# A chunked linear-attention stage: one list of steps over all heads in place of a loop over heads

## The reference, cut to what matters

```python
z = p[..., O_GA:O_RW] @ lp['w_gla_gate'] + lp['b_gla_gate']
la = (jax.nn.log_sigmoid(z.astype(f32)) / GLA_GATE_TAU)
def step(S, inp):                      # one chunk of 64 tokens
    qi, ki, vi, li = inp
    b = jnp.cumsum(li, axis=2)
    bl = b[:, :, -1:, :]
    qe = qi * jnp.exp(b)
    A = jnp.einsum('bhcd,bhsd->bhcs', qe, ki * jnp.exp(-b))
    A = jnp.where(mask, A, 0.0)
    o = jnp.einsum('bhcd,bhde->bhce', qe, S) + jnp.einsum('bhcs,bhse->bhce', A, vi)
    S = jnp.exp(bl[:, :, 0, :])[..., None] * S + jnp.einsum('bhsd,bhse->bhde', ki * jnp.exp(bl - b), vi)
    return S, o
og = og * lax.rsqrt(jnp.mean(og * og, axis=-1, keepdims=True) + GLA_NORM_EPS)
og = og.reshape(B, T, GLA_VW).astype(h.dtype) * lp['g_gla_norm'] * jax.nn.silu(gg)
```

## Time and profile before

| | us |
|---|---|
| median of 3 runs | 5423.79 |
| lowest, highest | 5419.95, 5428.64 |
| the profiled execution | 5427.57 |
| its span, first to last instruction | 5425.8 |
| from the first instruction of gla to the first of rwkv | 356.1 |

### The profile page before, as it was taken

How to read it: one execution, slowest core, us unless ns; L and a number is a source line. 1 busy time by engine, 2 the same in 40 slices (tenths; PEclk the granted TensorE clock), 3 DMA queues, 4 the chain that set the end, 5 groups by cost and what they waited for, 6 DMA issues and landing times. The chain is left out here.

```text
span 5425.8 us, 80977 instructions
## 1 busy us (share of the span) xinstructions
PE 4506.1 (83%) x30972; PEld 3060.4 (56%) x30972; DVE 3376.8 (62%) x6700; ACT 1090.8 (20%) x2093; POOL 1667.9 (31%) x1412
## 2 busy tenths in 40 slices
PE   8899998665887778799797764999899999999980
PEld 1899997553666667565387763444344443434430
DVE  0423332334555555311297664999999999999998
ACT  2100000332333333212433322011110111010101
POOL 0000000000111111000013334666566566656666
PEclk9999999667988888899898877999999999999985
DMA  5222222212000000231402224999999999999998
GB/s 221 83 94 94 93 91 102 73 67 67 24 24 28 24 24 19 102 122 59 151 25 79 76 71 162 394 378 378 339 384 375 367 359 379 386 344 384 362 348 299
DMA packets 354226, 1010.83 MB, mean 186 GB/s; under 512 B 39486, under 2 KB 120318, under 8 KB 349410
## 3 DMA queue, kind: packets, MB, share of 16 engines
q0 software_dynamic: 156672, 570.49, 26.9%
q1 hardware_dynamic: 197228, 435.98, 22.5%
HBM read 902.35 MB, written 103.99 MB: 185 GB/s over the span
## 5 line engine op out<-in xcount | busy, mean ns | idle before, releaser
L2611 PE MATMUL peer_v_b<-peer_vt,peer_mix 128*128 128x512 f32 x2048 | 943.1, 615 | 127.1 <-DVE peer_mix L2448 82.2
L2599 PE MATMUL peer_s_b<-dense_hT_d,peer_ut 128*128 128x512 f32 x2048 | 900.9, 593 | 51.5 <-DMA peer_G2s<-mod 51.5
L2384 POOL DMA_INDIRECT peer_ring<-in_peer_v,peer_idx x544 | 717.2, 1318 | 291.1 <-issue 160.6
L2611 PEld LDWEIGHTS peer_v_b<-peer_vt,peer_mix 128*128 128x128 f32 x2048 | 401.9, 198 | 652.5 <-issue 498.4
L2378 POOL DMA_INDIRECT peer_ring<-in_peer_u,peer_idx x544 | 597.3, 1098 | 487.4 <-DVE peer_acc L2500 229.9
L1367 POOL TENSOR_TENSOR rw_An<-rw_abT,rw_join 128x256 f32<-128x256 f32 x160 | 126.1, 795 | 1934.2 <-DVE rw_abT L1277 1545.0
L2599 PEld LDWEIGHTS peer_s_b<-dense_hT_d,peer_ut 128*128 128x128 f32 x2048 | 389.7, 190 | 542.0 <-issue 490.3
L2500 DVE SCALAR_TENSOR_TENSOR peer_acc<-peer_ring,peer_coef,peer_acc 128x1024 f32<-128x1024 f32 x534 | 653.9, 1279 | 0.0
L2537 DVE CUSTOM_DVE_ANT_0 peer_ring<-peer_ring,peer_h 128x1024 f32<-128x1024 f32 x544 | 637.2, 1218 | 2.0 <-DVE peer_h L2514 1.0
L56 PE MATMUL proj_acc<-proj_hT_high,proj_w_low 128*128 128x352 f32 x1584 | 512.3, 323 | 25.6 <-DVEq L363 25.6
L57 PE MATMUL proj_acc<-proj_hT_low,proj_w_high 128*128 128x352 f32 x1584 | 508.7, 321 | 0.0
(11 more groups left out here) (418 smaller groups left out, 6816.1 us busy)
## 6 DMA issues: line engine op xcount, KB each, us to landing
peer_ut<-in_peer_ut SPq DMA_DIRECT2D x128, 512.0 KB, 9.9
peer_vt<-in_peer_v SPq DMA_DIRECT2D x128, 512.0 KB, 8.0
pT<-proj_o SPq DMA_DIRECT2D x66, 528.0 KB, 3.0
proj_w<-in_w_in SPq DMA_DIRECT2D x66, 512.0 KB, 4.2
G<-route_G SPq DMA_DIRECT2D x16, 2048.0 KB, 16.4
peer_gt<-G SPq DMA_DIRECT2D x128, 256.0 KB, 6.0
mod_w<-in_w_ada SPq DMA_DIRECT2D x12, 2048.0 KB, 8.3
peer_ring<-in_peer_u,peer_idx POOLq DMA_INDIRECT x544, 10.3
```

Of the source, the lines that this page charges most:

```text
L2384: pool.indirect_dma_start(out=ring[:, k, :], out_offset=None, in_=t["peer_v"], in_offset=bass.IndirectOffsetOnAxis(ap=idx[U % 2][:, k:k + ...
L2599: last = pe.matmul(s_b[:, n % 3, :], ut[:, n % UT, k, :], hT_d[:, k, :], start=(k == 0), stop=(k == KD - 1))
L2611: last = pe.matmul(v_b[:, m % 4, :], mix[:, part % 2, e, tokens], vt[:, part % 2, e, cols], start=(e == 0), stop=(e == PART - 1))
```

## The change

The GLA stage becomes one list of steps over all four heads, made by `gla_steps` from a string of letters, and all four engines go through that same list, each taking the steps that it has a part in. Five streams are woven: t (turn a tile), s (its states), o (its output), p (the next head's preparation) and e (the last head's samples and end). Between the tiles of head h stand the preparation of head h + 1 and samples, sums of squares, root and og of head h - 1; head 0's preparation comes ahead, head 3's end behind. The list for a middle head, read out of the string:

```diff
+GLA_ORDER = (
+    "eptepstoestoepetspoeetesoeteseepoetesetepososeop",
+)
+def gla_steps():
+    def prepare(h):
+        return ([("z", h, g) for g in range(3)] + [(kind, h, 0) for kind in ("soft", "sums", "exps", "expand")]) if h < GH else []
+    def end(h):
+        if h < 0:
+            return []
+        return ([("turn", h, TILES), ("o", h, TILES), ("ks", h, 0)] + [("ss", h, b) for b in range(NB)] + [("sq", h, 0)]
+                + [("ms", h, g) for g in range(3)] + [("rstd", h, 0), ("og", h, 0)])
+    def stream(which, h):
+        return {"t": [("turn", h, i) for i in range(TILES)], "s": [("st", h, i) for i in range(TILES)],
+                "o": [("o", h, i) for i in range(TILES)], "p": prepare(h + 1), "e": end(h - 1)}[which]
+    relative = lambda which, h: [(kind, head - h, x) for kind, head, x in stream(which, h)]
+    whole = {which: iter(relative(which, 1)) for which in "tsope"}
+    turns = [(which, next(whole[which])) for which in "".join(GLA_ORDER)]
+    steps = prepare(0)
+    for h in range(GH):
+        have = {which: relative(which, h) for which in "tsope"}
+        steps += [(kind, head + h, x) for which, (kind, head, x) in turns if (kind, head, x) in have[which]]
+    return steps + end(GH - 1)
...
-        vg_next = s.sb("vg_next", [P, 4, M])
-        v, gate = s.sb("v", [P, 2, M]), s.sb("gate", [P, 2, M])
+        vg = [s.sb(f"vg{n}", [P, 4, M]) for n in range(2)]
         S_in = s.sb("S_in", [P, NB, GV])
         S_out = s.sb("S_out", [P, NB, GV])
         z = s.sb("z", [P, M])
         sp_ = s.sb("softplus", [P, M])
         B = s.sb("B", [P, M])
         up, dn, rest = s.sb("exp_up", [P, M]), s.sb("exp_down", [P, M]), s.sb("exp_rest", [P, M])
-        ends = s.sb("ends", [P, SEQ // GC + NB])
-        qe, ke, k2 = s.sb("qe", [P, M]), s.sb("ke", [P, M]), s.sb("k2", [P, M])
+        ends = s.sb("ends", [P, 2, SEQ // GC + NB])
+        qe, ke, k2 = ([s.sb(f"{name}{n}", [P, M]) for n in range(2)] for name in ("qe", "ke", "k2"))
         S = s.sb("S", [P, 4, GV])
-        kv = s.sb("kv", [P, 2, 3 * P])
+        kv, kv_s = s.sb("kv", [P, 3, 3 * P]), s.sb("kv_s", [NS, 3 * P])
         k2s = s.sb("k2s", [NS, NB, P])
         at = s.sb("at", [P, 2, P])
-        o, og = s.sb("o", [P, 2, M]), s.sb("og", [P, 2, M])
+        o = [s.sb(f"o{n}", [P, 2, M]) for n in range(2)]
+        og = s.sb("og", [P, 2, M])
+        sq, sig, rstd = s.sb("sq", [P, 2, M]), s.sb("sig", [P, 2, M]), s.sb("rstd", [P, M])
         ones = s.sb("ones", [P, P])
         eps = s.sb("eps", [P, 1])
-        sq = s.sb("sq", [P, 2 * M])
-        zb = s.ps("zb", [P, 3, 512])
-        at_b = s.ps("at_b")
-        turn_b = s.ps("turn_b")
-        o_b = s.ps("o_b")
-        s_b = [s.ps(f"s_b{n}") for n in range(2)]
-        N = TILES + 1
+        tb, o_b, s_b = (s.ps(name, [P, 2, 512]) for name in ("tb", "o_b", "s_b"))
+        zb, at_b = s.ps("zb"), s.ps("at_b")
...
+        def turned_kv(h, i):
+            return kv[:, (h * TILES + i) % 3, :] if i < TILES else kv_s
+        def kv_before(h, i):
+            if i == TILES:
+                return (h - 1, TILES) if h else None
+            n = h * TILES + i - 3
+            return divmod(n, TILES) if n >= 0 else None
...
+                sp.dma_start(gaT[:, :], t["gaT"]).then_inc(consts_in, 16)
+                sp.dma_start(wz[:, :, :], t["w_gate"].rearrange("h r p -> r h p")).then_inc(consts_in, 16)
+                sp.dma_start(cst[:, :, :], t["gla_cst"].rearrange("h p n -> p h n")).then_inc(consts_in, 16)
+                sp.dma_start(starts[:, :], t["starts"][:, 0:M].broadcast_to([P, M])).then_inc(consts_in, 16)
                 load_qk(0)
                 load_vg(0)
+                for dst, name in ((ident, "ident"), (mask, "gla_mask"), (mask_s, "gla_mask_s"), (seq_rows, "seq_rows")):
+                    sp.dma_start(dst[:, :], t[name]).then_inc(consts_in, 16)
+                load_vg(1)
                 load_states(0)
-                with sp.Fori(0, GH - 1) as h:
-                    head(h, True)
-                head(GH - 1, False)
-                sp.wait_ge(stored, 16 * 2 * GH)
+                sp.wait_ge(scaled, 3)
+                load_qk(1)
+                for h in range(GH):
+                    if h:
+                        sp.wait_ge(S_ready, state_at(h - 1, CH + NB - 1))
+                        sp.dma_start(t["new_gla_s"][h - 1], S_out[:, :, :]).then_inc(s_stored, 16)
+                        sp.wait_ge(o_summed, upto("o", h - 1, TILES))
+                        load_states(h)
+                        sp.wait_ge(og_ready, h)
+                        sp.dma_start(t["ogT"][h - 1], og[:, :, :]).then_inc(og_stored, 16)
+                        if h + 1 < GH:
+                            load_vg(h + 1)
+                    if h + 2 < GH:
+                        sp.wait_ge(scaled, 3 * (h + 2))
+                        load_qk(h + 2)
+                    sp.wait_ge(S_ready, state_at(h, CH - 1))
+                    sp.dma_start(t["new_gla_p"][h], S[:, CH % 4, :]).then_inc(p_stored, 16)
+                sp.wait_ge(S_ready, state_at(GH - 1, CH + NB - 1))
+                sp.dma_start(t["new_gla_s"][GH - 1], S_out[:, :, :]).then_inc(s_stored, 16)
+                sp.wait_ge(og_ready, GH)
+                sp.dma_start(t["ogT"][GH - 1], og[:, :, :]).then_inc(og_stored, 16)
...
+                    elif kind == "turn":
+                        n = upto("turn", h, x) - 1
+                        rows = P if x < TILES else NS
+                        act.wait_ge(turned, n + 1)
+                        before = kv_before(h, x)
+                        if before:
+                            act.wait_ge(o_summed, upto("o", *before))
+                            act.wait_ge(s_summed, last_state(*before))
+                        act.copy(turned_kv(h, x)[0:rows, :], tb[0:rows, n % 2, 0:3 * P]).then_inc(kv_ready, 1)
+                    elif kind == "o":
+                        n = upto("o", h, x) - 1
+                        rows = P if x < TILES else NS
+                        act.wait_ge(o_summed, n + 1)
+                        if h >= 2:
+                            act.wait_ge(og_ready, h - 1)
+                        act.copy(o[h % 2][:, :, x * P:x * P + rows],
+                                 o_b[:, n % 2, 0:2 * rows].rearrange("p (a c) -> p a c", a=2)).then_inc(o_ready, 1)
+                    elif kind == "sq":
+                        act.wait_ge(o_ready, upto("o", h, TILES))
+                        if h:
+                            act.wait_ge(ms_summed, 3 * h)
+                        act.activation(sq[:, :, :], o[h % 2][:, :, :], ACT.Square).then_inc(squares_ready, 1)
+                    elif kind == "ms":
+                        act.wait_ge(ms_summed, 3 * h + x + 1)
+                        if h:
                             act.wait_ge(og_ready, h)
-                        if i == 0:
-                            act.copy(gate[:, :, :], vg_next[:, 2:4, :]).then_inc(gate_kept, 1)
-                        if more and i in PREP:
-                            prep(PREP[i], h + 1)
-                    copy_o(h, N - 1)
-                    act.wait_ge(o_ready, h * N + N)
-                    act.activation(sq[:, :], o[:, :, :].rearrange("p a m -> p (a m)"), ACT.Square).then_inc(squares_ready, 1)
-                    if more:
-                        act.wait_ge(S_ready, (h + 1) * (US + 1))
-                        expand(h + 1)
-                    act.wait_ge(ms_summed, h + 1)
-                    ch.link(act.activation(z[:, :].rearrange("p (g c) -> p g c", g=3), zb[:, :, 0:G3], ACT.Ln, bias=eps[:, :]))
-                    act.activation(z[:, :], z[:, :], ACT.Exp, scale=-0.5)
-                    act.wait_ge(gate_kept, h + 1)
-                    act.activation(sq[:, :], gate[:, :, :].rearrange("p a m -> p (a m)"), ACT.Sigmoid).then_inc(rstd_ready, 1)
-
-                def copy_o(h, i):
-                    act.wait_ge(o_summed, h * N + i + 1)
-                    rows = P if i < TILES else NS
-                    act.copy(o[:, :, i * P:i * P + rows],
-                             o_b[:, 0:2 * rows].rearrange("p (a c) -> p a c", a=2)).then_inc(o_ready, 1)
-
-                prep("softplus", 0)
-                prep("exps", 0)
-                expand(0)
-                ch.enter(0, 3)
-                head(0, True, True)
-                ch.leave(1)
-                with act.Fori(1, GH - 1) as h:
-                    ch.enter(h - 1, 3)
-                    head(h, False, True)
-                    ch.leave(GH - 2)
-                head(GH - 1, False, False)
+                        act.activation(rstd[:, g_cols(x)], zb[:, 0:G3], ACT.Ln,
+                                       bias=eps[:, :]).then_inc(ms_read, 1)
+                    elif kind == "rstd":
+                        act.wait_ge(ms_read, 3 * (h + 1))
+                        act.activation(rstd[:, :], rstd[:, :], ACT.Exp, scale=-0.5)
```

(54 more changed lines are left out.)

378 lines of the change are left out of this document (151 added, 227 removed).

## The result

The changed kernel takes 5377.94 us (median of 4 runs, 5371.03 to 5384.10) against 5421.87 for the kernel before on the same chip (4 runs, 5408.24 to 5428.64): a ratio of 0.9922, 95% interval 0.9898 to 0.9945. The forecast was 5359, range 5325 to 5410, faster at 0.9. So the sign and the range hold, and of the 65 us of gain forecast 44 came.

The account below looks back on a forecast made before the run. Waits, and a slower TensorE clock after them, were taken to bound the stage. Its terms, 37.5 + 37.4 + 63.6 + 63.6 + 51.2 + 37.8 = 291 against 356.1 us, gain 65: 5359 us, range 5325 to 5410.

Parts of the forecast that it names:

- Start: Stage start up to the first head's first turn: from 31.9 to about 37.5 us, waiting for const loads behind 2.1 MB more.
- Head 0: First head, its tiles cleared of most other work: 31 us at the high clock level, 47 at the low, 37.4 taken.
- The point two fifths of the way from the fast end: Clock level chosen between the all-high sum of 256 us and the all-low 343 for the stage: 291.
- Heads 1 and 2: Middle heads carrying all five streams: 54 us each at the high clock level, 78 at the low, 63.6 taken.
- (a): ScalarE at a middle head's boundary: copy, rstd, sigmoid, then exponentials; 10 us without an output copy, o7 needing o5's bank.
- (b): VectorE's og at a middle head's boundary, after the sigmoid: 7.5 us, with expand and the next head's masks behind it.
- (c): SP's v and gate loads for the next head, issued only behind og: about 10.7 us before its first turn.
- The tail: Last head's samples' output, ms, rstd, og and store: today's 37.8 us, three-part ms saving a wait, paying two round trips.
- Rival 1: TensorE stays at 1.2 GHz nearly throughout the stage: 13 us less, 5411, covering 5395 to 5420; chance 0.13.
- Table loads: ScalarE's two loads ahead of og: 1.28 us each by the row; the skill's 2.66 would add 2.8 per boundary.
- 3: Rival: the streams do not run beside each other, stalls only move; stage 325, gain 31 us, 5393; chance 0.16.
- 2: Rival: v/gate loads at two head boundaries make it slower, at 23 us each and low clock 5435; chance 0.05.

Follow-up runs that it names:

- kernel tail: Changed kernel with mask loads ahead of q, k, v and gate, and the last head's sums of squares in three banks ahead of six sample states: 5362.78 us.
- v_x: v_early with the next head's exponentials moved behind the states of tile 7, out of ScalarE's block: 5362.77 us.
- e_first: Changed kernel with only the order string rearranged, the last head's samples and end ahead of all the next head's tiles: 5405.09 us.
- p_last: Changed kernel with only the order string rearranged, the next head's whole preparation behind the head's tiles, samples and end of the last head: 5403.64 us.
- v_early: Changed kernel with v of the next head loaded once the last head's samples' turn has read the buffer, gate still behind og: 5362.09 us.

## Why the prediction held, and where it was off

- **Start**: 37.9 for 37.5, and z at 941.8 for "near 941". The extra loads ahead of the last constants are the cost, as the kernel tail shows by taking them away.
- **Head 0**: 37.0 for 37.4, at a clock of 0.73 over the head. The sums' stall was 3.46 against "3.5 or 1.4"; the exponentials cost nothing, as said, and expand nothing, the lower of its two prices. Head 3: 51.2 for 51.2. The point two fifths of the way from the fast end was a choice, and here a good one; that both agree so closely is luck.
- **Heads 1 and 2**: 69.4 and 63.1 for 63.6 each. (a) o7 waits for o5's bank, 6.8 in each (2.4 in head 3, where no exponentials stand there); (b) og takes 7.4 (1053.53 to 1060.89); (c) the landing came 10.4 behind the store, for 10.7. The 5.8 of head 1 are the clock, 0.65 for head 2's 0.74 with the same steps. The sum had charged (b) and (c) behind rstd and sigmoid and nothing for o7, 24.2 from the end of turn 7, and it took 23.9 (1047.43 to 1071.32). That was right, for (a) and (b) are one chain: freeing ScalarE from the one only moves the wait (v_x). Two terms in it were loose. Five outputs at the rows' 2.74 are 13.7 and not 12.8, which is under 1 us a head, and about 1 of the 10.7 for the landing is a start-up that no row gives.
- **The tail**: 43.6 for "today's, 37.8". This is the term that was mis-sized: three rounds through one bank, and TensorE at 1.2 GHz throughout (clock 0.50, before 0.63), so the samples' output takes 6.99 us (4.87 in the kernel before's tail) and the sums 9.55 (5.71 before, in one block). From the tail's start to the sample states it is 2.6 us more, and from the sums to the load of the next table 3.3 more; together they make up the 5.9. I had taken the saving and the round trips as a draw, and the clock as unchanged. The sum had also named og ahead of the samples' output as a price of head 3, but not what the standstill does to the clock behind it. The Trainium skill (TensorE: Matmul & The Clock Gate, section A second HAM failure mode: psum-queue depth-cycling) tells of a kernel whose clock swings between its two levels because TensorE idles briefly between groups of matmuls. No run here shows that by itself: the sums have 8.07 us of matmuls with two gaps of 0.74 between them, against 6.1 for the twelve without a gap in the kernel tail, but the order was changed there too, and in the changed kernel the 18 us from the samples' output to the end of the first group, which lie ahead of both gaps, were at the low level as well.
- **The stage**: 302.2 for 291, 5.8 from head 1 and 5.8 from the tail; the mean clock was 0.66, where I had said above 0.7. Rival 1 in its strong form is out (5377.9 against its 5395 to 5420). A clock lower than I took, in head 1 and the tail, is behind much of the stage's miss; that short idles cause it, as the rival's milder form says, is not shown.
- **Table loads**: 1212.56 - 1211.27 is 1.29 us from a load's start to the next activation's, so the row's price held, and not the 2.66 us per switch, drain included, that the Trainium skill (ScalarE: Activation LUTs, section What ACT_TABLE_LOAD costs) gives.
- **"Later stages unchanged to within 3 us"**: this failed, with 10.9 in the rwkv stage of the profiled execution, 6.6 in the second, where the kernel before alone has 999 to 1010 in its three profiles. It is the second half of the miss: 5363 forecast for that execution, 5384.1 found, 21 us: 11 in the stage, 11 in rwkv, and 1 less in all the rest. I had taken an unedited stage for a constant; its work is, its clock isn't.
- **Rivals**: 3 falls (e_first, p_last), 2 has its mechanism at under half of its deciding price (10.4 us for 23, v_early), 1 is as above.
